# Latent attention in three fp32r products, with the next pair's projections between the units of this pair

## What is computed

```python
def mla_keys_values(ckv, kpe, w_ukv):
    kv = (ckv @ w_ukv).reshape(b, t, MLA_HEADS, MLA_NOPE + MLA_V)
    k_pe = jnp.broadcast_to(kpe[:, :, None, :], (b, t, MLA_HEADS, MLA_ROPE))
    return jnp.concatenate([kv[..., :MLA_NOPE], k_pe], axis=-1), kv[..., MLA_NOPE:]
...
def mla_latent(h, ctx_cache, w_in, q_norm_g, kv_norm_g, w_uq, w_ukv, w_o):
    q, ckv, kpe = mla_project(h, w_in, q_norm_g, kv_norm_g, w_uq)
    q = concatenate([q[..., :MLA_NOPE], apply_axial_rope(q[..., MLA_NOPE:], ang_r, ang_c)])
    kpe = apply_axial_rope(kpe, ang_r, ang_c)
    ...                                   # keys and values of latent and cached tokens
    o = block_attention(q, k, v).reshape(b, t, MLA_HEADS * MLA_V)   # softmax(q k / sqrt(192)) v
    return o @ w_o
```

## Time and profile before

| | |
|---|---|
| median of the runs | 2342.36 us |
| profiled execution | 2341.09 us, span 2339.4 us |
| PE, DVE, ACT busy in the span | 87%, 48%, 40% |
| the four pairs together | 346.1 us (240.1 to 586.2 in the span) |
| PE, DVE, ACT busy in the four pairs | 324.7, 113.5, 79.9 us |

### The profile page before, as it was taken

The page is one execution under the profiler, slowest core; times in us unless marked ns, Lnnn a source line. Parts: engine busy times, 40 slices in busy tenths (PEclk is TensorE's granted clock), DMA queues, the critical chain, the costliest instruction groups (busy, mean ns, idle before and its releaser), DMA issues. The chain is left out here.

```text
span 2339.4 us, 25523 instructions
## 1 busy us (share of the span) xinstructions
PE 2039.0 (87%) x8674; PEld 1416.1 (61%) x8674; DVE 1129.5 (48%) x1603; ACT 928.6 (40%) x1288; POOL 112.3 (5%) x131
## 2 busy tenths in 40 slices
PE   5669899999489999839999999999999939999974
PEld 2235454554368888628756765875675427888853
DVE  1132324323479999753232422323242248999965
ACT  1021212311378888632211221222121137888854
POOL 0000000000100000011000100100010010000001
PEclk8879999898689999959999999999999969999986
DMA  9967000100789999461221220221110078999933
GB/s 374 409 229 324 22 28 11 35 18 0 293 288 399 399 399 398 170 243 37 81 63 39 74 84 18 85 79 51 67 41 18 20 294 315 399 398 398 399 140 122
DMA packets 169029, 424.81 MB, mean 182 GB/s; under 512 B 10621, under 2 KB 22426, under 8 KB 168986
## 3 DMA queue, kind: packets, MB, share of 16 engines
q1 hardware_dynamic: 152624, 365.44, 42.1%
q0 software_dynamic: 10944, 39.85, 4.5%
q10 hardware_dynamic: 5418, 18.96, 2.0%
HBM read 369.01 MB, written 55.21 MB: 181 GB/s over the span
## 5 line engine op out<-in xcount | busy, mean ns | idle before, releaser
L1776 DVE TENSOR_TENSOR moe_w_lo<-weight_ring,moe_w_hi 128x1024 fp32r<-128x1024 f32 x432 | 518.2, 1223 | 102.4 <-ACT moe_w_hi L1708 88.7
L1708 ACT ACTIVATE moe_w_hi<-weight_ring 128x1024 fp32r<-128x1024 f32 x432 | 454.8, 1065 | 156.6 <-PE ps L1641 108.0
L1641 PE MATMUL ps<-moe_w_hi,moe_rows_t_hi 128*128 128x512 f32 x576 | 232.8, 404 | 5.1 <-DVE moe_rows_t_lo L1781 4.7
L1239 DVE TENSOR_TENSOR ret_w_lo<-weight_ring,ret_w_hi 128x512 fp32r<-128x512 f32 x128 | 95.9, 749 | 286.0 <-ACT ret_w_hi L1175 286.0
L1641 PE MATMUL ps<-moe_w_hi,moe_rows_t_lo 128*128 128x512 f32 x576 | 226.5, 393 | 0.0
L1641 PE MATMUL ps<-moe_w_lo,moe_rows_t_hi 128*128 128x512 f32 x576 | 226.3, 393 | 0.0
L1175 ACT ACTIVATE ret_w_hi<-weight_ring 128x512 fp32r<-128x512 f32 x128 | 80.6, 633 | 309.1 <-PE ps L1052 309.1
L1052 PE MATMUL ps<-ret_w_hi,h_hi 128*128 128x512 f32 x480 | 194.0, 404 | 3.4 <-ACT weight_ring L1179 2.1
L1052 PE MATMUL ps<-ret_w_lo,h_hi 128*128 128x512 f32 x480 | 189.6, 395 | 0.0
L1052 PE MATMUL ps<-ret_w_hi,h_lo 128*128 128x512 f32 x480 | 189.6, 395 | 0.0
L1641 PE MATMUL ps<-moe_w_hi,moe_hidden_t_hi 128*128 128x512 f32 x288 | 117.6, 408 | 9.7 <-DVE moe_hidden_t_lo L1786 8.0
(11 more groups left out here) (283 smaller groups left out, 2922.2 us busy)
## 6 DMA issues: line engine op xcount, KB each, us to landing
weight_ring<-in_moe_w_gate SPq DMA_DIRECT2D x36, 2048.0 KB, 12.9
weight_ring<-in_moe_w_up SPq DMA_DIRECT2D x36, 2048.0 KB, 15.0
weight_ring<-in_moe_w_down SPq DMA_DIRECT2D x36, 2048.0 KB, 15.2
weight_ring<-in_ada_w SPq DMA_DIRECT2D x24, 2048.0 KB, 23.9
weight_ring<-in_ret_w_in SPq DMA_DIRECT2D x12, 2048.0 KB, 8.6
h_normed<-rows_in POOLq DMA_DIRECT2D x36, 512.0 KB, 7.1
rows_out<-h_normed ACTq DMA_DIRECT2D x36, 512.0 KB, 6.3
rows_in<-zero_rows SPq DMA_DIRECT2D x26, 512.0 KB, 8.0
```

What stands on the lines that cost most here:

```text
L1239: dve.tensor_tensor(wlo[:, n % BUF, :], win[s][:, k, :], whi[:, n % BUF, :].bitcast(F32), ALU.subtract).then_inc(w_lo, 1)
L1641: mm = pe.matmul(out, lhs, rhs, start=(first and x == 0), stop=(last and x == 2))
L1708: nc.scalar.activation(whi[:, x, :], part(u, w + x), ACT.Identity).then_inc(w_hi, 1)
L1776: dve.tensor_tensor(wlo[:, x, :], part(blk[1], w + x), whi[:, x, :].bitcast(F32), ALU.subtract).then_inc(w_lo, 1)
```

## The change

Every product of the pairs, but for the swap, the transposes and O, becomes three fp32r matmuls: each operand is split in a high part, which ScalarE writes as fp32r, and a low part, which VectorE makes as the difference (high x high, high x low, low x high). The latents are split once, at the end of `mla_project`. Weights are split for each pair: wq (1152 columns), wkv (1024) and wo (four quarters of 512), and so are q, k, the attention output o and the rotary queries.

The rotary scores are stacked: head hd's high part of the rotary query stands on its own 64 partitions and its low part on the other 64 (`mla_qpe_stack`, moved there by two DMAs on POOL's queue), so that one 128-row product with the doubled key gives both; two of them, with the key's high and low part, replace the 64-row product. Columns are cut in even halves (2 x 320) instead of 128 + 512, and the context unit's scores are made 256 wide, of which 128 are read.

The loop over pairs is written out. The next pair's q0, k0, qp, qs, q1 and k1 stand behind the transposes of units 4 to 9 of this pair; its v0 to v2, S0 and S1 stand between O1 and w0. O0 moves from behind unit 8 to behind unit 5. The weights of later pairs are loaded as soon as their slot has been split.

```diff
 def mla_project(c, m, j):
+                act.wait_ge(dve_n.sem, dve_n.value("n21"))
+                nc.scalar.activation(m["cq"][0][:, :, :], cq[:, :, :], ACT.Identity).then_inc(act_s, 1)
                 take(5)
+                ...                                   # ckv, kpe the same way
+                def low(name):
+                    dve.wait_ge(act_n.sem, act_n.value("h" + name))
+                    dve.tensor_tensor(m[name][1][:], full[:], m[name][0][:].bitcast(F32), ALU.subtract).then_inc(dve_s, 1)
 def mla_pairs(c, m, layer, j):
+    LATER = {4: ["q0"], 5: ["O0", "k0"], 6: ["qp"], 7: ["qs"], 8: ["q1"], 9: ["k1"]}
+    for i in range(PAIRS):
+        for u in range(NU):
+            order += ([f"S{u + 2}.{i}"] if u + 2 < NU else []) + [f"T{u}.{i}"]
+            order += [f"{n}.{i if n == 'O0' else i + 1}" for n in LATER.get(u, ()) if n == "O0" or i + 1 < PAIRS]
+        order += [f"O1.{i}"] + [f"{n}.{i + 1}" for n in ("v0", "v1", "v2", "S0", "S1") if i + 1 < PAIRS]
+        order += [f"w{d}.{i}" for d in range(KD)]
+    bank = {n: 2 * (g % 4) for g, n in enumerate(order)}
...
+                    for hd in range(2):                # POOL, one time per pair
+                        pool.dma_start(stack[(1 - hd) * ROPE:(2 - hd) * ROPE, hd, :], qlo[hd * ROPE:(hd + 1) * ROPE, :]).then_inc(stack_s, 16)
...
+                def three(out, left, right, first, last):
+                    for x, (l, r) in enumerate(((0, 0), (0, 1), (1, 0))):
+                        mm = pe.matmul(out, left(l), right(r), start=(first and x == 0), stop=(last and x == 2))
+                    return mm
...
                 def scores(u, i):
-                        pe.matmul(ps[:, b + r, 0:n], q[:, hd, cols], k[:, hd, a:a + n], start=True, stop=False)
-                        mm = pe.matmul(ps[:, b + r, 0:n], qpe[half, cols], kpe[half, a:a + n], start=False, stop=True)
+                        three(out, lambda x: q[x][:, hd, cols], lambda x: k[x][:, hd, a:a + n], True, False)
+                        for x in range(2):
+                            mm = pe.matmul(out, stack[:, hd, cols], kpe[x][:, a:a + n], start=False, stop=(x == 1))
...
+                for i in range(PAIRS):                 # VectorE
+                    for u in range(1, NU):
+                        if u + 1 < NU:
+                            maximum(u + 1, i)
+                        normalise(u, i)
+                        take_last(u - 1, i)
+                        if u in (1, 2):
+                            split(f"o{2 * u - 2}", i)
+                            split(f"o{2 * u - 1}", i)
+                        if i == 0 and u == 3:
+                            split("q", 1)
+                        if i == 0 and u == 4:
+                            split("kv", 1)
+                        if u == 6:
+                            low_o(0, i)
+                        if more and u == 5:
+                            low_q(0, i + 1)
+                        ...                            # k0 at 6, rotate at 8, rotary low parts and q1 at 9
```

More of the change, by code:

```diff
@@ L554, in _ @@
                 dve.tensor_copy(rows[:, :], ps[:, 7, 0:3 * P]).then_inc(dve_s, 1)
+                low("ckv")
+                low("kpe")
 def mla_slots(c):
@@ L604, in mla_pairs @@
[L604 to L616, removed]
-    with ExitStack() as st:
[L618 to L624, removed]
+    NU, HALF, QUARTER = len(UNITS), T // 2, D // 2
@@ new lines, in keys @@
+                def keys(hd, i):
+                    if hd == 0:
+                        dve_n.wait(pe, f"lkv.{i}")
+                    take_bank(f"k{hd}.{i}")
+                    for r in range(2):
+                        cols = slice(r * KEYS // 2, (r + 1) * KEYS // 2)
+                        for b in range(2):
+                            mm = three(flat_ps(f"k{hd}.{i}", 128 + r * KEYS // 2, KEYS // 2), lambda x: wkvp[x][:, b, hd, 0:NOPE],
+                                       lambda x: ckv[x][:, b, cols], b == 0, b == 1)
+                    mm.then_inc(done, 1)
@@ new lines, in swapped, with values @@
+                def swapped(i):
+                    act_n.wait(pe, f"qp.{i}")
+                    take_bank(f"qs.{i}")
+                    pe.matmul(ps[:, bank[f"qs.{i}"], :], m["swap"], qraw[:, SEQ:T], start=True, stop=True).then_inc(done, 1)
+                def values(g, i):
+                    take_bank(f"v{g}.{i}")
+                    for r in range(2):
+                        t = 2 * g + r
+                        for b in range(2):
+                            mm = three(ps[:, bank[f"v{g}.{i}"] + r, 0:2 * VD], lambda x: ckv[x][:, b, t * P:(t + 1) * P],
+                                       lambda x: wkvp[x][:, b, :, NOPE:2 * NOPE], b == 0, b == 1)
+                    mm.then_inc(done, 1)
@@ new lines, in output @@
+                def output(d, i):
+                    if d == 0:
+                        dve_n.wait(pe, f"lo3.{i}")
+                        dve_n.wait(pe, f"O1.{i}")
+                    take_bank(f"w{d}.{i}")
+                    for r in range(2):
+                        for hd in range(2):
+                            mm = three(flat_ps(f"w{d}.{i}", 192 + r * HALF, HALF), lambda x: wop[x][:, hd, d * P:(d + 1) * P],
+                                       lambda x: o[x][:, hd, r * HALF:(r + 1) * HALF], hd == 0, hd == 1)
+                    mm.then_inc(done, 1)
@@ L737, in _ @@
+                query("q0", 0)
+                keys(0, 0)
+                query("qp", 0)
+                swapped(0)
+                query("q1", 0)
+                keys(1, 0)
+                scores(0, 0)
+                scores(1, 0)
+                for g in range(3):
+                    values(g, 0)
+                for i in range(PAIRS):
+                    more = i + 1 < PAIRS
                     for u in range(NU):
@@ new lines, in _ @@
+                        if more and u == 5:
+                            keys(0, i + 1)
+                        if more and u == 6:
+                            query("qp", i + 1)
+                        if more and u == 7:
+                            swapped(i + 1)
+                        if more and u == 8:
+                            query("q1", i + 1)
+                        if more and u == 9:
+                            keys(1, i + 1)
+                    attend(1, i)
+                    if more:
+                        for g in range(3):
+                            values(g, i + 1)
+                        scores(0, i + 1)
+                        scores(1, i + 1)
@@ new lines, in take_last @@
+                    if t:
+                        prod.wait(dve, f"T{u}.{i}")
+                        dve.tensor_copy(pt[:, hd, 4, (t - 1) * P:t * P], ps[:, bank[f"T{u}.{i}"] + 1, 0:P]).then_inc(dve_s, 1)
+                split("q", 0)
+                split("kv", 0)
+                low_q(0, 0)
+                low_k(0, 0)
+                rotate(0)
+                low_q(1, 0)
+                low_k(1, 0)
+                low_qpe(0)
+                maximum(0, 0)
+                maximum(1, 0)
@@ L855, in _ @@
                                                      op0=ALU.mult, op1=ALU.add).then_inc(dve_s, 1)
+                        if d == 1 and more:
+                            normalise(0, i + 1)
+                        if d in (3, 5) and i + 2 < PAIRS:
+                            split("q" if d == 3 else "kv", i + 2)
 QK, V, F, B = 0, KD, 2 * KD, 3 * KD
```

502 lines of the change are left out of this document (332 added, 170 removed).

## The result

The changed kernel takes 2284.72 us (median of 4 runs, 2283.84 to 2288.25); its time is 0.9727 of the time before, with an interval from 0.9656 to 0.9798. Forecast were 2293 us. The profiled execution took 2284.48 us with a span of 2281.6, so the span fell by 57.8 us, where 48.1 were forecast.

The account below looks back on a forecast made before the run. PE was taken as the bound. 5.0 + 30.8 + 200.7 + 51.5 = 288.0 us against 346.1, 58.1 less; minus 10 for the clock, 2341.1 - 48.1 = 2293.0 us, range for 8 in 10 2274 to 2316.

Parts of the forecast that it names:

- first product later: Start of the stage: low parts of cq, ckv, kpe and wq's halves come first, PE begins 5.0 us later.
- pair 1's opening: Pair 1 before S2: projections, splits, stacking DMAs, S0, S1 and values take 30.8 us, where it was 27.6.
- last pair: From the last pair's S2 to the stage's end, without projections to fill with: 51.5 us at the upper level.
- PE's work: Products of one pair at the upper level keep PE busy 58.8 us, where pair 2 had 77.6.
- waits elsewhere: PE's waits before the swap, T8, T9 and O1: 1.3 us a pair.
- the loads stand bare: Rival, all new 128-row products: weight loads don't overlap, 120 us more, 2413 us; chance 0.02.
- The 0.2 us a couple: Old scores: 64-row products cost some 0.2 us a couple beyond their streaming, and those go.
- The stall before T2 and T3: Rounds 1 and 2: wo's splits on VectorE and ScalarE make PE stand about 6.0 us a pair.
- The clock: Unit loop: gaps lower the clock, 2.5 us a pair, 10 in all; rival, it holds: 2283 us, chance 0.18.
- 2.4 us for the splits of wq and wkv: Pair 1, rounds 3 and 4: splitting the second wq and wkv adds 2.4 us.
- The chain as the bound of all rounds: Rival: from scores to transposes, up to 1 us more in some 20 of 40 rounds, 2313 us; chance 0.17.
- the 25 us named: Sign: the forecast is wrong if the lower clock level covers more than some 25 us of the stage.

Follow-up runs that it names:

- wo split in round 5: Changed kernel with wo's four quarters split in round 5 instead of rounds 1 and 2: 2264.1 us, ratio 0.9631 to the kernel before.
- the filled waits: Changed kernel with 10 and 18 useless products of 320 columns put ahead of T2 and T3: 2277.8 us, ratio 0.9688 to the kernel before.
- values ahead of S0: Changed kernel with pair 1's three value products moved from behind S0 and S1 to ahead of them: 2276.5 us, ratio 0.9707 to the kernel before.

## Why the prediction was right, and where its sizes were off

The forecast's terms with the clock's share put to each, against the trace:

| Term | forecast us | measured us |
|---|---|---|
| first product later | 5.0 | 4.8 |
| pair 1's opening | 30.8 | 34.5 |
| pair 1 | 71.0 | 66.3 |
| pairs 2 and 3 | 137.2 | 132.1 |
| last pair | 54.0 | 52.3 |
| sum | 298.0 | 290.1 |

The number came closer than its parts: pairs and end were 11.5 us too long, and the opening 3.7 too short. Pair 2 in the terms of the forecast (PE's work, stall, waits elsewhere, clock): 58.4 + 4.6 + 0.4 + 3.0 = 66.4, where 58.8 + 6.0 + 1.3 + 2.5 = 68.6 had been put.

**PE's work.** Forecast 58.8 us a pair; busy are 58.4 where the clock stays up (wo split in round 5). This term carries the result, and it held. Waits elsewhere in a pair are 0.36 us, before T8, where 1.3 had been counted.

**The weight loads.** Of the rival "the loads stand bare" nothing came. In this trace the loads of 128-row products take 188 ns each (the 128 of each kind in w), and the products start 0.147 us apart, so they lie beside other work. The Trainium skill (TensorE: Matmul & The Clock Gate, Part 3, The mechanism) has a load overlap only with products of another row group, though the same section also lets one that goes to the background weight buffer be pulled ahead; the first, taken alone, the trace contradicts for 128-row products by these 0.147 us. In the run with 64-row products each change of the row count cost 0.2 us, and an unchanged row count nothing. The 0.2 us a couple that the prediction read from the earlier trace rows is of the same size, with one change to a couple (its 0.53 us are four times 320 columns at 0.133, not two). In fp32 without such changes the price is not there: the output projection in fp32, 64 instructions on 128 rows, takes 17.39 us, 0.54 a couple. That it goes with the stacking was right.

**The stall before T2 and T3.** The place and the cause held: both runs that took wo's splits from there took T3's wait away in pairs 2 and 3, and T2's but for 0.63 us. The size was 4.6 us in pair 2 (0.20, 1.61 and 2.83 before T1, T2, T3) and not 6.0. The prediction's chain from S2's end to T3 was 10.95 us; it took 9.96 (347.25 to 357.21). Its three rounds took 4.06, 4.17 and 1.73 us, not 4.4, 4.6 and 1.95. It had added whole durations from the earlier trace rows, 0.63 and 0.69 us for a part; two parts together take 1.16 and 1.29, and the next instruction starts before the shown end of the last (351.31 against 350.10 + 1.29).

**The clock.** 2.5 us a pair was right for pair 2 (2.7 by the filled waits) and wrong for pair 1, where it is 0; over all pairs the filled waits gave back 6.9 (6.1 in the trace of the stage), not 10. There the prediction added it to 2.4 us for the splits of wq and wkv. Either fits alone, 2.09 us for the wait when the clock stays up; together they share one wait. This double count, some 2 us, and the stall's size, 1.4 us a pair, are most of the 9.8 us that the three pairs came out shorter.

**The opening** was 3.7 us too short. The stacking DMAs took 3.9 us from the lows' end (265.1) to S0 instead of 2.8, inside the bounds of 1.8 to 5. S0, S1 and the values took 10.4 instead of 8.2, part of it S2's wait of 1.46 us for an exponential queued behind value copies, which the prediction had not seen.

**The chain as the bound of all rounds**: T1, T2 and T8 keep 0.2 to 0.63 us each without any split, some 1.2 us a pair, so the margin was thin, but rounds 3 to 7 of a filled pair don't wait.

**What would show it**: the signs named came, and with them one that was to show the forecast wrong. The lower level covers more than the 25 us named: the granted clocks of the stage's rows from the first product on (0.77 to 0.97) come to some 36 us at 0.50, some 28 of them with PE at work. The time held all the same: 11 of these 28 us lie in q0 and in S0 to the values, where the forecast had counted the lower level in part, and those in pair 1 cost nothing.

## What to carry to other kernels

When an engine gets faster, look for work that stays in front of its feeders: moving one split by three or four rounds gave 20.6 us, a third of what the whole change had given. Put such work where the fast engine has a long piece of its own, and count a wait and a clock fall behind the same instruction once. Keep the row count of successive products the same.

## What had not been expected

Idle time alone does not tell when the level falls. A gap of 3.08 us before S0 (values ahead of S0) was followed by products at the upper level, one of 2.02 before T3 (wo split in round 5) by the lower. And in pair 1 of the kernel with 64-row products the level stayed low while PE was busy without a break:

```profile
286.00:290.00 4.00, 4.00 (x13) 2.91 (x12) 2.75 (x6) 2.09 (x5) 0.00 (x0) 0.50 0.00 0
...
302.00:306.00 4.00, 4.00 (x16) 3.34 (x16) 2.67 (x6) 1.78 (x4) 0.00 (x0) 0.50 0.68 182
```

It began at 285.4, with no idle time of 0.15 us or more shown since 282.98, where S2 had waited 1.47 us, and lasted some 23 us. What starts it stays open; the runs show only that where the splits' waits before T2 and T3 were gone or filled, it did not come in pairs 2 and 3.
